# A two-layer diffusion block on one core: scan operands transposed ahead, the two scan directions in step, a last projection with fewer columns, and routing by halves

## The chip, the core and the metric

The kernel runs on one core of a Trainium2 chip. The metric is the device time of one execution in microseconds (us). The core has a matrix engine (TensorE, PE in the profile, with PEld for its weight loads), VectorE (DVE), ScalarE (ACT), GpSimd (POOL), and SyncE (SP), which only issues DMAs here. Each engine runs its own instructions strictly in the order in which they are written and waits on semaphores for the others.

## What is computed

Two layers (`l` = 0, 1) over 256 context tokens and 1024 latent tokens of width 1024, all in float32. Each layer projects the normalised tokens with `w_in`, runs four mixers side by side (a short convolution, an attention, a two-way RWKV scan and a two-way retention), projects back with `w_out`, and then sends each token set through 16 experts, each of which picks its own tokens. After the last layer only the latent tokens are returned, so there `need_ctx` is false: of the context, only what the mixers carry over to the latent tokens matters. The parts that the change touches, cut from the reference:

```python
def step(s, inp):                         # the scan, per token, in both directions
    w_t, a_t, k_t, v_t, kk_t = inp[:5]
    s = (s * w_t - einsum('bhvk,bhk->bhv', s, kk_t) * (kk_t * a_t) + v_t * k_t)
    y = einsum('bhvk,bhk->bhv', s, inp[5]) if emit else None

s_fw, yc_fw = wkv_scan(s0, *dc[0], vc, kkc, rc, False, need_ctx)   # context first
_, yx_fw = wkv_scan(s_fw, *dx[0], vx, kkx, rx, False, True)        # then the latent tokens

aff = softmax(hs @ w_router + b_router)   # routing
gate, idx = lax.top_k(aff.T, cap)         # cap = 128 of 1024 latent, 32 of 256 context
```

## The kernel before

Tokens lie in 10 tiles of 128 (`NT`): tiles 0 and 1 are context (`NCT` = 2), 2 to 9 latent. A stage is one block; all engines meet at its end. A layer is: norm, `stage_project`, attention, retention, and twice (for `p` = 0, 1, two heads each) `stage_rwkv_prep`, `stage_rwkv_scan`, `stage_rwkv_out`; then `stage_out`, `stage_topk`, `stage_moe`.

**Projection.** A job is one output tile, eight matmuls deep. Of groups "conv" and "rwkv" the weights are stationary and the tokens stream past in three spans (256, 512, 512 columns). Of group "tok" the tokens are stationary and 272 or 512 weight columns stream past, a job for each of the 10 token tiles. ACT evacuates even jobs, DVE odd ones. DVE also mixes each rwkv tile with its neighbours in time (`mix`, L553 to L562): `mix(i)` is written after the last job that DVE evacuates of tile `i + 1`, and `mix(7)` ends the stage. Both layers do the same jobs.

**Preparation of the scan.** Its tail is a loop of 15 rounds over both directions: a matmul against a constant (`spread`, L1343) copies 16x16 block rows across partitions, and DVE multiplies and subtracts (L1427, L1432) to invert these blocks. DVE waits for the matmuls, PE only for its ring of banks.

**Scan.** For each of 10 tiles and each direction `d` there are two kinds of work. The *inversion* of a tile needs no state: `products` (PE), `masked` (DVE, writes `UM`), the masks `NL` (POOL), `transposes` (PE, L1546: four operands by token, 16 small matmuls against the identity), `by_token` (ACT, copies them to `TM`), then twice `level_x` (PE), `x_out` (ACT), `level_t` (PE and DVE), and at last `w1_w2` (PE) and `w_out` (ACT, L1702 and L1704). The *carry* of the tile before takes the state through two halves of 64 tokens: `carry_u` and `carry_s`, each PE then DVE. `products` of the next tile waits for `w_out`, since they share banks. The order is written by hand: a tile takes 7 slots, and direction 1 runs 3 slots behind direction 0.

```python
SLOTS, LAG = 7, (0, 3)
def slots():
    for q in range(SLOTS * (NT + 1) + LAG[1]):
        yield [(d, *divmod(q - LAG[d], SLOTS)) for d in DD if 0 <= q - LAG[d] < SLOTS * (NT + 1)]
```

`level_x` waits for three signals: the mask of POOL, the block inverse in `TS`, and `tme`, the copy of ACT (`by_token`).

**Routing.** `g.aff` holds the affinities as 16 experts by 1280 tokens. `stage_topk` takes the 128 largest of 1024 in 16 rounds on DVE, each of which finds the 8 largest, finds their places and strikes them out. In layer 0 it then takes 32 of the 256 context tokens in 4 rounds. PE turns indices and values, and DVE copies them to `g.tok` and `g.gate`. In the same stage SP issues the loads of the first 8 expert weight parts (2 MB each).

## Time and profile before

| | us |
|---|---|
| median of three runs | 4874.7 (4870.68 to 4875.51) |
| the profiled execution | 4870.7 |
| its span, first to last instruction | 4868.8 |
| projection of layer 1 (PE, first to last matmul) | 2641.5 to 3099.3 |
| the four scans | 118.9, 118.9, 119.2, 120.5 |
| DVE in the rounds of routing, layer 0 / layer 1 | 1612.7 to 1681.0 / 4086.8 to 4148.8 |

A float32 matmul runs as two records in the trace, so 8 matmuls are "x16"; a transpose of 128x128 runs as one. A duration of a record ("mean ns of one") holds its latency as well; what PE spends on one in a row of many is their busy time by their count, or the distance of two starts. Rows of a timeline are start, duration, engine, line and tiles, and in brackets how long the engine had been idle and whose result ended that.

### The profile page before, as it was taken

To read this page: it belongs to the slowest core of one execution; us is meant where nothing else is said; L and a number is where in the kernel's file an instruction comes from. 1 tells how busy PE (TensorE), PEld (TensorE's weight loads), DVE (VectorE), ACT (ScalarE), POOL (GpSimd) and SP (SyncE) were. 2 spreads that over 40 slices of the span, in tenths; PEclk is the share of its full clock that TensorE was granted. 3 is DMA by queue.
4 is the path that set the end of the run, shared out by engine and by line. 5 is a ranking of instruction groups with operands and counts; after the bars stand their busy time and mean duration, and the time that the engine had idled before them with its cause. 6 is when DMAs were issued, how large, how long until landed. Compare 5 with 4: busy or idle time off the path is not lost. (4 is left out here: it accounts for less than half of the span.)

```text
span 4868.8 us, 64424 instructions
## 1 busy us (share of the span) xinstructions
PE 4017.1 (83%) x27764; PEld 2253.6 (46%) x27764; DVE 1579.1 (32%) x3277; ACT 793.1 (16%) x1792; POOL 450.7 (9%) x662
## 2 busy tenths in 40 slices
PE   6999688457779399999996999677466885899999
PEld 3645245445644144444443655344454742344444
DVE  2101454765633600000002101454666536100000
ACT  2000243133211000000002010243133210000000
POOL 0000100021200000001000000100021200000000
PEclk8999889688889599999997999789678987899999
DMA  4110400100045466677753110000100034688884
GB/s 151 62 72 11 138 34 10 50 20 16 3 176 222 171 229 229 243 264 259 262 186 84 59 71 16 26 3 22 45 12 16 3 126 181 240 312 309 311 327 161
DMA packets 196074, 624.94 MB, mean 128 GB/s; under 512 B 34473, under 2 KB 47017, under 8 KB 189137
## 3 DMA queue, kind: packets, MB, share of 16 engines
q1 hardware_dynamic: 173200, 548.13, 30.1%
q0 software_dynamic: 22592, 72.69, 4.9%
q8 instruction: 221, 3.62, 0.3%
q14 instruction: 61, 0.49, 0.0%
HBM read 566.90 MB, written 53.89 MB: 128 GB/s over the span
## 5 line engine op out<-in xcount | busy, mean ns | idle before, releaser
L484 PE MATMUL ps<-hT,p_w 128*128 128x512 f32 (+1 forms) x1344 | 486.2, 525 | 19.2 <-DMA p_w<-in_w_in_dram 19.2
L2177 PE MATMUL ps<-moe_w,e_xT 128*128 128x512 f32 x1024 | 451.2, 599 | 0.8 <-ACT e_xT L2239 0.8
L2214 PE MATMUL ps<-moe_w,e_hT 128*128 128x512 f32 x1024 | 445.9, 593 | 6.1 <-ACT e_hT L2258 6.1
L2184 PE MATMUL ps<-moe_w,e_xT 128*128 128x512 f32 x1024 | 444.7, 592 | 0.0
L487 PE MATMUL ps<-p_w,hT 128*128 128x272 f32 (+1 forms) x1280 | 422.3, 492 | 0.0
L484 PEld LDWEIGHTS ps<-hT,p_w 128*128 128x128 f32 x1344 | 258.1, 192 | 246.0 <-issue 213.3
L487 PEld LDWEIGHTS ps<-p_w,hT 128*128 128x128 f32 x1280 | 243.2, 190 | 178.9 <-issue 154.0
L2280 DVE TENSOR_TENSOR e_hid<-e_hid,ps 128x512 f32<-128x512 f32 x64 | 44.0, 688 | 838.6 <-PE ps L2184 838.6
L2177 PEld LDWEIGHTS ps<-moe_w,e_xT 128*128 128x128 f32 x1024 | 195.0, 192 | 247.2 <-issue 245.9
L2184 PEld LDWEIGHTS ps<-moe_w,e_xT 128*128 128x128 f32 x1024 | 194.6, 190 | 244.9 <-issue 244.9
L2214 PEld LDWEIGHTS ps<-moe_w,e_hT 128*128 128x128 f32 x1024 | 192.0, 190 | 239.0 <-issue 239.0
L1881 PE MATMUL ps<-o_w,yT 128*128 128x512 f32 x576 | 261.2, 608 | 29.6 <-DMA o_w<-in_w_out_dram 24.5
L860 PE MATMUL ps<-mla_KT,mla_QT 96*128 96x512 f32 (+1 forms) x400 | 181.8, 540 | 6.6 <-ACT a_pr L984 4.6
L1881 PEld LDWEIGHTS ps<-o_w,yT 128*128 128x128 f32 x576 | 109.3, 194 | 166.2 <-issue 133.1
L2290 DVE SCALAR_TENSOR_TENSOR e_ye<-ps,all_gate,e_rows 128x1024 f32<-128x1024 f32 x32 | 41.1, 1283 | 427.2 <-PE ps L2214 427.2
L2251 ACT ACTIVATE e_hid<-ps 128x512 f32<-128x512 f32 x64 | 34.7, 594 | 716.4 <-PE ps L2177 716.4
L570 DVE COPY p_zo<-ps 128x272 f32<-128x272 f32 (+1 forms) x40 | 22.7, 566 | 366.7 <-PE ps L487 366.7
L872 PEld LDWEIGHTS ps<-all_tabs,a_pr 128*128 128x128 f32 x656 | 74.4, 142 | 127.6 <-issue 86.6
L872 PE MATMUL ps<-all_tabs,a_pr 128*128 128x128 f32 x656 | 111.4, 283 | 19.3 <-ACT a_pt L929 13.8
L950 DVE TENSOR_REDUCE a_mx<-ps 128x1 f32<-128x1280 f32 (+1 forms) x72 | 98.5, 1368 | 54.4 <-PE ps L860 54.4
L2193 PE MATMUL ps<-moe_w,e_xTc 128*32 128x512 f32 x1024 | 113.2, 594 | 0.0
L2049 PE MATMUL ps<-all_tabs,k_idf 16*128 16x16 f32 (+1 forms) x3 | 0.8, 257 | 132.2 <-DVE k_idf L2034 132.2
(328 smaller groups left out, 5555.1 us busy)
## 6 DMA issues: line engine op xcount, KB each, us to landing
moe_w<-in_w_gate_dram SPq DMA_DIRECT2D x64, 2048.0 KB, 13.3
moe_w<-in_w_up_dram SPq DMA_DIRECT2D x64, 2048.0 KB, 11.0
moe_w<-in_w_down_dram SPq DMA_DIRECT2D x64, 2048.0 KB, 16.9
o_mod_w<-in_w_ada_dram SPq DMA_DIRECT2D x24, 1024.0 KB, 11.1
p_w<-in_w_in_dram SPq DMA_DIRECT2D x10, 2048.0 KB, 8.0
m_mod_w<-in_w_ada_dram SPq DMA_DIRECT2D x16, 1024.0 KB, 6.6
z_rows<-p_zo POOLq DMA_DIRECT2D x40, 256.0 KB, 2.3
r_z<-z_rows SPq DMA_DIRECT2D x20, 512.0 KB, 3.3
```

Source lines behind the costliest of these rows:

```text
L484: ins = nc.tensor.matmul(ps[:, j % NB, 0:tw], w[:, n % RW, k, m * P:(m + 1) * P], hT[:, k, t0:t0 + tw], start=(k == 0), stop=(k == KT - 1))
L487: ins = nc.tensor.matmul(ps[:, j % NB, 0:wd], hT[:, k, m * P:(m + 1) * P], w[:, n % RW, k, 0:wd], start=(k == 0), stop=(k == KT - 1))
L860: ins = nc.tensor.matmul(ps[:, SB[u % 2] + i, 0:w], QT[0:QK, h, t * P:(t + 1) * P], KTr[0:QK, h, n:n + w], start=True, stop=True)
L872: ins = nc.tensor.transpose(ps[:, TB, k * P:(k + 1) * P], pr[:, u % NP, (k0 + k) * P:(k0 + k + 1) * P], g.ident)
L950: link(nc.vector.reduce_max(mx[:, s % 2, 0:1], src, AX_X))
L1881: ins = nc.tensor.matmul(ps[:, 2 * (n % 2) + half, :], yT[:, k, t * P:(t + 1) * P], w[:, k, half * 512:(half + 1) * 512], start=(k == 0), ...
L2177: ins = nc.tensor.matmul(ps[:, c, :], xT[:, 4 * half + k], wp[:, k, c * 512:(c + 1) * 512], start=(half == 0 and k == 0), stop=(half == 1 ...
L2184: ins = nc.tensor.matmul(ps[:, 2 + c, :], xT[:, 4 * half + k], wp[:, k, c * 512:(c + 1) * 512], start=(half == 0 and k == 0), stop=(half = ...
L2193: ins = nc.tensor.matmul(ps[32 * q:32 * q + 32, 4, :], xTc[:, 4 * half + k], (wg, wu)[q // 2][:, k, (q % 2) * 512:(q % 2 + 1) * 512], star ...
L2214: ins = nc.tensor.matmul(ps[:, 6 + c, :], hT2[:, 4 * half + k], wp[:, k, c * 512:(c + 1) * 512], start=(half == 0 and k == 0), stop=(half ...
L2280: nc.vector.tensor_tensor(hid[:, h], hid[:, h], ps[:, 2 + c], ALU.mult).then_inc(*hd.up())
L2290: nc.vector.scalar_tensor_tensor(ye[:, e % 2], bank(ps, 6, D), g.gate[:, 0, e:e + 1], rows[:], ALU.mult, ALU.mult).then_inc(*yd.up())
```

## The change

Three parts, which touch no common stage.

**Projection of the last layer.** With `need_ctx` false, context tokens are left out where nothing reads them. The first span (256 columns) falls away for all 6 conv tiles and for rwkv tiles 0, 1 and 7. In the "tok" groups the two context tiles lose group 2 whole, keep 160 of 272 columns in group 3, and 256 of 512 in groups 4 and 5. POOL writes zeros into the context part of the conv tiles. `mix` takes the last job of its tile, wherever that is.

**Scan.** The four operands by token (three for direction 1; it shares the fourth) are made by 70 full transposes of 128x128 in the tail of the preparation, between the spread matmuls, into `BYTOK`, which lies where buffers of the preparation are free by then; ACT copies them out, 20 copies. In the scan `transposes` and `by_token` are gone, and both directions go through the same six slots together. `decayed` and `y_out` are written apart from the carries.

**Routing.** The affinities lie in rows of 512: the two halves of the latent tokens on partitions 0 to 15 and 32 to 47, the context on 64 to 79. The 16 rounds run on all of these rows at once; the 4 context rounds are gone. Then PE turns values and indices, the second half's list is reversed by a matmul against `flip`, and DVE merges the two lists with a maximum and a choice by comparison.

```diff
+    ctx_cols = {2: None, 3: (112, 272), 4: (256, 512), 5: (0, 256)}
+    ctx_tiles = range(2, 7)
...
-            jobs += [(n, m, s) for m in range(w // P) for s in range(3)]
+            jobs += [(n, m, s) for m in range(w // P) for s in range(3) if s or need_ctx or (kind == "rwkv" and o + m in ctx_tiles)]
...
-                    last = rw0 + 3 * i + 2
+                    last = max(j for j in range(rw0, len(jobs)) if tile_of(j) == i)
...
+            def by_token(u):
+                d, t = units[u]
+                if u >= 4:
+                    pe.wait_ge(*tok_out.at(u - 3))
+                for a, src in enumerate(sources(d)):
+                    ins = nc.tensor.transpose(ps[:, TBANKS[u % 4], a * P:(a + 1) * P], src[:, t * P:(t + 1) * P], g.ident)
+                ins.then_inc(*turned.up())
...
+                for u in range(len(units) * n // (DB - 1), len(units) * (n + 1) // (DB - 1)):
+                    by_token(u)
...
+            act.wait_ge(*ksd.at(1))
+            for u, (d, t) in enumerate(units):
+                act.wait_ge(*turned.at(u + 1))
+                w = len(sources(d)) * P
+                nc.scalar.copy(BT[d][:, t].rearrange("p a n -> p (a n)"), ps[:, TBANKS[u % 4], 0:w]).then_inc(*tok_out.up())
...
-                for now in slots():
...
+                for s in range(NT + 1):
+                    inv, car = s < NT, s > 0
+                    for d in DD:
+                        if car:
+                            w1_w2(d, s - 1)
+                    for d in DD:
+                        if inv:
+                            products(d, s)
+                        if car:
+                            carry_u(d, s - 1, 0)
+                    for d in DD:
+                        if inv:
+                            m_v(d, s)
+                        if car:
+                            carry_s(d, s - 1, 0)
+                        if inv:
+                            level_x(d, s, 0)
+                    for d in DD:
+                        if inv:
+                            level_t(d, s, 0)
+                        if car:
+                            carry_u(d, s - 1, 1)
+                    if inv:
+                        level_x(0, s, 1)
+                    if car:
+                        carry_s(0, s - 1, 1)
+                    if inv:
+                        level_x(1, s, 1)
+                        level_t(0, s, 1)
+                    if car:
+                        carry_s(1, s - 1, 1)
+                    if inv:
+                        level_t(1, s, 1)
...
+                for r in range(CAPX // 8):
+                    v8 = val[:, 8 * r:8 * r + 8]
+                    link(nc.vector.max(v8, a))
+                    link(nc.vector.max_index(idx[:, 8 * r:8 * r + 8], v8, a))
+                    link(nc.vector.match_replace(a, v8, a, -1.0))
...
+                nc.vector.tensor_tensor(g.gate[:, 0], tt[:, 0, A], ps[:, 1, 0:NE], ALU.max)
+                link(nc.vector.tensor_tensor(sel[:], tt[:, 0, A], ps[:, 1, 0:NE], ALU.is_ge))
+                link(nc.vector.tensor_tensor(dif[:], tt[:, 1, A], ps[:, 1, NE:2 * NE], ALU.subtract))
+                link(nc.vector.tensor_tensor(dif[:], dif[:], sel[:], ALU.mult))
+                link(nc.vector.tensor_tensor(dif[:], dif[:], ps[:, 1, NE:2 * NE], ALU.add))
+                nc.vector.tensor_copy(g.tok[:, 0], dif[:])
```

PE in the middle of a scan, before: `w1_w2` and the levels of one direction among the carries and transposes of the other (L1546 the transposes, L1556 `level_x`, L1574 `level_t`, L1537 `products`, L1524 and L1527 `carry_s`, L1509 and L1513 `carry_u`).

```order
L1537 MATMUL ps<-rw_KR,rw_BK 64x128 x8
L1556 MATMUL ps<-s_TS,s_NL 64x64 x4
L1524 MATMUL ps<-s_UM,s_TM 64x64 x2
L1527 MATMUL ps<-s_TM 64x64 x2
L1524 MATMUL ps<-s_UM,s_U 64x64 x2
L1527 MATMUL ps<-s_U,s_TM 64x64 x2
L1546 MATMUL ps<-all_tabs,rw_KR 64x64 x4
L1546 MATMUL ps<-all_tabs,rw_BK 64x64 x8
L1546 MATMUL ps<-all_tabs,M 64x64 x4
L1574 MATMUL ps<-s_TS,s_X 64x64 x4
```

The same engine and place after the change (L1571 `products`, L1543 and L1547 `carry_u`, L1588 `m_v`, L1558 and L1561 `carry_s`, L1580 `level_x`; `rp_wide` holds the operands by token).

```order
L1571 MATMUL ps<-rw_KR,rw_BK 64x128 x8
L1543 MATMUL ps<-s_S,s_W 64x64 x2
L1547 MATMUL ps<-rw_KR,s_S 64x64 x2
L1588 MATMUL ps<-rp_wide,s_UM 64x64 x4
L1558 MATMUL ps<-s_UM,rp_wide 64x64 x2
L1561 MATMUL ps<-rp_wide 64x64 x2
L1558 MATMUL ps<-s_UM,s_U 64x64 x2
L1561 MATMUL ps<-s_U,rp_wide 64x64 x2
L1580 MATMUL ps<-s_TS,s_NL 64x64 x4
L1588 MATMUL ps<-rp_wide,s_UM 64x64 x4
```

The transposes are gone, and the second direction's `m_v` now stands right behind the first direction's `level_x`.

PE in the tail of the preparation, before: the spread matmuls stand in a row.

```order
L1331 MATMUL ps<-rw_KR,rw_BK 32x32 x160
L1343 MATMUL ps<-rp_GX,rp_SG 128x300 x2
L1343 MATMUL ps<-rp_GX,rp_SG 128x280 x2
L1343 MATMUL ps<-rp_GX,rp_SG 128x260 x2
L1343 MATMUL ps<-rp_GX,rp_SG 128x240 x2
```

The same place after the change (L1374 the spread matmuls, L1341 the transposes).

```order
L1374 MATMUL ps<-ro_GX,ro_SG 128x300 x2
L1341 MATMUL ps<-all_tabs,rw_KR 128x128
L1341 MATMUL ps<-all_tabs,rw_BK 128x128 x2
L1341 MATMUL ps<-all_tabs,M 128x128
L1374 MATMUL ps<-ro_GX,ro_SG 128x280 x2
L1341 MATMUL ps<-all_tabs,rw_KR 128x128
L1341 MATMUL ps<-all_tabs,rw_BK 128x128 x2
L1374 MATMUL ps<-ro_GX,ro_SG 128x260 x2
```

Between two pairs of spread matmuls there are now three to seven transposes.

## Rows read from the trace of the kernel before

**Rows 1.** Groups by line and shape, 2580 to 3120 us; count, busy us, mean ns
```profile
L484 PE MATMUL ps<-hT,p_w 128*128 128x512 f32 x448 | 194.5, 592 | 0.0
L487 PE MATMUL ps<-p_w,hT 128*128 128x512 f32 x320 | 137.7, 592 | 0.0
L487 PE MATMUL ps<-p_w,hT 128*128 128x272 f32 x320 | 73.7, 392 | 0.0
L484 PE MATMUL ps<-hT,p_w 128*128 128x256 f32 x224 | 52.8, 390 | 9.6 <-DMA p_w<-in_w_in_dram 9.6
```
**Rows 2.** Timelines of PE and of DVE at the end of layer 1's projection
```profile
2961.68 137.66 PE L484 MATMUL ps<-hT,p_w 128*128 128x256 f32 x384
...
3107.24 1.28 DVE L561 SCALAR_TENSOR_TENSOR M<-p_z,p_omu,p_tmp 128x1024 f32<-128x1024 f32 x1
```
**Rows 3.** Stretches of a scan: length, busy us by engine, clock share (1.00 is 2.4 GHz)
```profile
1080.00:1156.00 76.00, 64.68 (x2201) 59.63 (x2199) 44.60 (x154) 27.98 (x96) 20.58 (x56) 1.00 0.02 4
1049.00:1052.00 3.00, 1.92 (x47) 1.76 (x48) 0.45 (x2) 0.65 (x2) 1.42 (x4) 0.50 0.00 0
```
**Rows 4.** Timeline of DVE: the same instruction of one direction, one tile apart
```profile
1098.38 0.69 DVE L1647 TENSOR_TENSOR s_UM<-ps,rw_masks 128x512 f32<-128x512 f32 x1
...
1109.36 0.69 DVE L1647 TENSOR_TENSOR s_UM<-ps,rw_masks 128x512 f32<-128x512 f32 x1
```
**Rows 5.** Timeline of the engines from that mask to the first level
```profile
1099.15 0.87 POOL L1695 TENSOR_TENSOR s_NL<-s_UM,rw_nlev 128x128 f32<-128x128 f32 x2 [2.35 <-DVE s_UM L1647]
...
1099.89 0.59 ACT L1709 COPY s_TM<-ps 128x512 f32<-128x512 f32 x1 [0.54 <-PE ps L1546]
...
1100.62 0.45 PE L1556 MATMUL ps<-s_TS,s_NL 64*64 64x64 f32 x8 [0.35 <-ACT s_TM L1709]
```
**Rows 6.** Timeline of PE in a scan: starts of bursts that follow one another
```profile
1101.64 0.44 PE L1586 MATMUL ps<-s_MV,s_TS 64*64 64x64 f32 x8
1101.87 0.44 PE L1574 MATMUL ps<-s_X,s_TS 64*64 64x64 f32 x8
...
1103.07 0.33 PE L1537 MATMUL ps<-rw_KR,rw_BK 64*64 64x128 f32 x3
...
1103.57 0.44 PE L1556 MATMUL ps<-s_TS,s_NL 64*64 64x64 f32 x8
1103.84 0.33 PE L1524 MATMUL ps<-s_UM,s_TM 64*64 64x64 f32 x4
...
1104.24 0.28 PE L1527 MATMUL ps<-s_U,s_TM 64*64 64x64 f32 x4
```
**Rows 7.** Timeline of ACT: the last copies of w_out
```profile
1102.30 0.53 ACT L1704 COPY s_W<-ps 64x128 f32<-64x128 f32 x2
```
**Rows 8.** Timeline of DVE: the last update of the state in the first scan
```profile
1166.24 0.28 DVE L1633 SCALAR_TENSOR_TENSOR s_S<-ps,rw_ET,s_Se 128x64 f32<-128x64 f32 x1 [1.22 <-PE ps L1527]
```
**Rows 9.** Timelines of PE and DVE: start and end of the preparation's loop
```profile
1029.55 1.37 PE L1343 MATMUL ps<-rp_GX,rp_SG 128*128 128x300 f32 x2
...
1047.08 0.32 DVE L1432 TENSOR_TENSOR rw_TD<-rw_TD,rp_GX 128x20 f32<-128x20 f32 x2
```
**Rows 10.** Timeline of PE: eight transposes at the full clock, in the experts
```profile
4189.27 1.04 PE L2158 MATMUL ps<-all_tabs,e_xe 128*128 128x128 f32 x8
```
**Rows 11.** A stretch of layer 1's norm, where PE only transposes
```profile
2620.00:2630.00 10.00, 6.86 (x30) 5.26 (x28) 7.34 (x22) 9.13 (x22) 2.20 (x4) 0.50 0.29 101
```
**Rows 12.** Instructions on the affinities: duration ns min/median/max
```profile
L2030 DVE MAX8 k_val<-all_aff x36: 407/1216/1217, 1612.7 to 4144.9; 16x8 f32<-16x1024 f32 x32, 16x8 f32<-16x256 f32 x4
```
**Rows 13.** Timeline of DVE in layer 1's routing: one round, and the end
```profile
4086.75 1.22 DVE L2030 MAX8 k_val<-all_aff 16x8 f32<-16x1024 f32 x1 [0.32 <-PEq L1831]
...
4090.62 1.22 DVE L2030 MAX8 k_val<-all_aff 16x8 f32<-16x1024 f32 x1
...
4149.84 0.17 DVE L2038 COPY all_gate<-ps 128x16 f32<-128x16 f32 x1
```
**Rows 14.** A stretch of layer 1's routing; last two numbers: DMA share, GB/s
```profile
4125.00:4130.00 5.00, 0.00 (x0) 0.00 (x0) 4.86 (x7) 0.00 (x0) 0.00 (x0) 0.50 0.92 365
```

264 lines of the change are left out of this document (140 added, 124 removed).

## The prediction

> **What bounds the kernel now.** I read the busy shares in 40 slices first: PE is nearly full in both projections and both expert stages and lower between them, and the three parts of the change lie in stages that share nothing. So each of the three parts is costed in its own stage. Next come the groups by shape in the projection: PE streams without a gap, 434 ns for a record of 512 columns, 230 ns for one of 272 [rows 1]. Whatever columns go, their time goes. Then the stretches inside a scan: in 76 us PE is busy for 64.7, DVE for 44.6, at the full clock of 2.4 GHz [rows 3]. Neither is full; the same mask instruction of one direction comes back after 10.98 us, so a tile of both directions takes that long [rows 4]. Last the routing: DVE works alone there, and PE waits.
>
> **Projection of layer 1.** Removed are 9 jobs of 256 columns, 16 records each: 144 records. The group of 256 gives 52.8 / 224 = 236 ns, but it holds the cold start; from the 384 records of the rwkv groups, 137.66 us [rows 2], take 256 of 512 columns at 434 ns, and 128 are left with 26.6 us, 207 ns each. I take 215: 31.0 us. Two jobs of 272 columns: 32 x 0.230 = 7.4. Four jobs halved from 512: 64 x (0.430 - 0.215) = 13.8. Two jobs from 272 to 160: by columns a record would take 135 ns, and not less than the 110 of a full transpose below; I take 160, so 32 x 0.07 = 2.2. Sum 54.4 (50 to 58). The end shortens too. Before, DVE's last job was the last of all, and behind it stood both `mix(6)` and `mix(7)`: PE ends at 3099.3 and DVE at 3108.5 [rows 2], 9.2 us. Now the count of jobs is odd, DVE's last job lies one job (6.9 us) earlier, `mix(6)` (4.1 us) runs beneath PE's last job, and only `mix(7)` and a copy stay: about 4.9 us, 4.3 less. The zeros that POOL writes lie at the stage's start, before anything asks for them. **Projection: -58.7 us.** Its cover is nothing; PE is the bound.
>
> **The scan's step.** What goes is the transposes with their copy. The first level could start once POOL's first mask is there, half of 0.87 us after 1099.15, at 1099.6; it starts at 1100.62, having waited for ACT's copy, 0.59 us, which waited for the transposes [rows 5]. So each inversion loses 1 us of chain. What is late next is PE itself. The bursts' prices by the distance of starts [rows 6]: eight records of a level or of `m_v` 0.23 to 0.27, `products` 0.50, `carry_s` 0.52 (12 records in 0.40, and 4 more), `carry_u` 0.25, `w1_w2` 0.41 (half of it on four quarters of the array, half as a level). One direction of one tile now holds `w1_w2` 0.41, `products` 0.50, two `carry_u` 0.50, `m_v` 0.24, two `carry_s` 1.04, two `level_x` 0.54, `level_t` 0.47 and 0.24: 3.94 us. Both: 7.9 us, and a step can't be shorter. To that come the waits in PE's new order. The largest is at `products`: `w1_w2` of direction 0 must end (0.2 us behind its last start), ACT copies `w_out` in about 0.73 (0.53 of it the two last copies [rows 7]), and beneath it lies only `w1_w2` of direction 1: PE stands 0.4 to 0.6 us. I went through a step with these prices, 0.2 us from a burst's last start to its end and 0.05 us for each handover: elsewhere the other direction's burst covers each wait (for `masked` 0.69, for U, for X 0.27), with 0.1 left over here and there, and DVE, with 3.6 us for each direction, is just in time for `w1_w2` of direction 1. That gives 8.5; I take 8.6. From 10.97 to 8.6 are 2.37 us, for 9 full steps of 4 scans: 85.3 us.
>
> **The scan's ends.** The first scan runs from 1047.4 to 1166.5, 119.1 us [rows 8, 9]; less 9 steps of 10.97 its two ends take 20.4. The lag of 3 slots, 4.7 us, is part of it. New: a first step of inversions alone, at the half clock (0.50 in its second to fourth us [rows 3]), some 9.5 us, and a last one of carries alone, some 7: 16.5. Four times 3.9 is 15. **Scans: -100 us** (bounds: step 8.0 gives -122, step 9.4 gives -71).
>
> **The preparation's tail.** Added are 70 transposes of 128x128 per scan. Eight take 1.04 us with their latency [rows 10], so 0.11 each: 7.7 us of PE. The spread matmuls stream 4 records x 20 x (1 + ... + 15) = 9600 columns; at 0.434 / 512 = 0.85 ns that is 8.1 us, and 9.2 if the short ones cost no less than a transpose. Together 17 us at the full clock. The loop took 17.9 us with DVE as its bound, 1029.5 to 1047.4, and started at the half clock: its first two records, 300 columns each, take 1.37 us [rows 9]. With some 4 us of such a start PE needs about 20.5 us and becomes the bound. Behind it stands one copy of ACT (0.59 as in [rows 5]); the 20 copies, some 11 us, lie beside PE, and ACT is idle there. I take +4 per scan (0 to +14). **Preparation: +16 us.** The copies wait for POOL's sum of keys too, which is over ten us earlier.
>
> **Routing.** One round takes 4090.62 - 4086.75 = 3.87 us [rows 13]. The search takes 0.407 us on 256 columns and 1.216 on 1024 [rows 12], so by a straight line 0.68 on 512; the other two are alike. A round of 512 then takes 3.87 - 3 x 0.54 = 2.26, provided that 80 partitions cost as much as 16: the row says only that the time follows the columns. 16 rounds: -25.8 us in each layer. Layer 0 also loses its 4 context rounds, 5.9 us. Sixteen rounds end at 4148.7 and the copies at 4150.0 [rows 13], 1.3 us; now PE turns, DVE copies, PE reverses, and six small steps follow, about 3.5 in all; +2.2 in each layer, less 0.6 of separate context copies in layer 0, and three memsets ahead, +0.3. Layer 0: -29.5; layer 1: -23.3. SP's loads of weights start with the stage as before, behind one more small DMA, and still run until 4130 in layer 1 [rows 14]; the first gather would now start at 4126 and share the last 4 us with them, +1. **Routing: -51.8 us.**
>
> **The sum.** 4870.7 (the profiled execution, 4.0 below the median of the three) - 58.7 - 100 + 16 - 51.8 = 4676.2. I predict 4676.
>
> **Rivals.** (a) *PE alone sets the step.* The wait for `w_out` is filled by running ahead; step 7.9, 36 x 0.7 = 25 less: 4651. For it: PE can have its next burst ready. Against: `products` really needs the banks that `w_out` reads. (b) *A slot keeps its length.* 10.97 / 7 = 1.57 us; six are 9.4: +29, 4705. For it: in step both directions ask DVE for the same thing at once, and DVE would be at 7.2 of 9.4 us. Against: the slots before held the transposes, which were their longest wait. (c) *The tail of the preparation runs at 1.2 GHz.* In a stretch of layer 1's norm where PE only transposes, it is busy for 6.86 of 10 us and the granted clock stays at 0.50 [rows 11], where as busy a scan has 1.00 [rows 3]. If the transposes between them thin out the spread matmuls so far that the clock stays down, PE needs 2 x 17 us from its start at 1029.5, to 1063: +16 instead of +4; with part of the loop at the full clock I price it at +10 over the forecast in each, +40: 4716. For it: that row. Against: the spread matmuls alone have raised the clock so far, with gaps between them. The Trainium skill says in "TensorE: Matmul & The Clock Gate", Part 4, that a transpose in transpose mode doesn't count as PE being busy; by that rule, the norm's row agrees, and rival (c) would be what happens. (d) *The scan stays at 1.2 GHz.* Its first steps do, with both directions at work (0.50 [rows 3]). Were it to last, PE's 7.9 us would be 15.8 and a step 16.4: 36 x 7.8 = 281 more, 4957, slower than before. It decides from a step of 14.0 us on, where 36 x 5.4 eats the whole gain. Against: PE issues for nine tenths of a step, more than before. That the change doesn't do what it says could hold for the narrow jobs only (a record of 160 or 256 columns as dear as one of 272): +3.
>
> **How the numbers follow.** The forecast 0.58; (a) 0.10; (b) 0.15; (c) 0.10; (d) 0.02; something between or a mishap of a few us elsewhere 0.05. The range has (a) and the step of 8.0 near its lower end and (b) and most of (c) near its upper: 4645 to 4718. All but (d) lie far below 4870, so faster has 0.97, slower 0.02, and within 0.2% (about what a measurement of this kernel can tell from no change) 0.01.
>
> **What would show it.** In the trace after: the mask of one direction comes back after 8.6 us (7.9, 9.4 or over 14 for the rivals); the wait of `level_x` for ACT is gone, and the largest waits of PE in a scan stand at `products` for `w_out`; the loop of the preparation ends 4 us later, with the granted clock at 1.00 in its middle (0.50 by (c)); DVE's MAX8 takes 0.68 us; PE's stretch in layer 1's projection is 54 us shorter. Wrong would be made most easily the step, since 36 of them stand in the sum: each 0.1 us is 3.6.

## The result and the profile after

The changed kernel takes 4644.9 us (median of 4 runs, 4635.1 to 4646.2), beside 4875.1 for the kernel before in the same series: a ratio of 0.9523, 95% interval 0.9507 to 0.9540. The prediction was 4676 with a range of 4645 to 4718, so the time lies 31 us below the forecast and 0.1 us below the range's lower end. A second series gave 4632.8 (5 runs, 4629.3 to 4640.4) beside 4872.5, 0.9512 (0.9499 to 0.9525). So the direction and three of the four terms held, and the fourth, the scans, gave 37 us more than priced.

The profiled execution is the run of 4645.8 us, 224.9 less than that of before. By stage (us, from DVE's and PE's timelines of both traces):

| part | predicted | measured | from |
|---|---|---|---|
| projection of layer 1 | -58.7 | -59.7 | PE's stretch 457.9 to 402.4, its end 9.2 to 5.0 |
| the steps of the scans | -85.3 | -107 | step 10.97 to a mean of 7.99, 36 of them |
| the ends of the scans | -15 | -30 | 20.5 to 13.1, four of them |
| the preparation's tail, with the gap to the scan | +16 | +15.1 | +3.6, +3.3, +5.6, +2.7, from the end of DVE's last product of the preparation to the scan's first instruction |
| routing | -51.8 | -49.6 | layer 0 -27.9, layer 1 -21.8 |
| everything else | 0 | +6.3 | the largest are the output stage of layer 0 (+4.1) and the attention of layer 1 (+3) |

**The projection.** Timelines of PE and of DVE at its end, after; they answer to [rows 2].

```profile
2835.01 127.30 PE L494 MATMUL ps<-hT,p_w 128*128 128x512 f32 x336
```
```profile
2955.53 0.69 DVE L582 COPY p_z<-ps 128x512 f32<-128x512 f32 x1 [8.88 <-PE ps L494]
...
2963.02 1.50 DVE L570 TENSOR_TENSOR p_tmp<-p_z 128x1282 f32<-128x1282 f32 x1 [2.63 <-ACT p_z L514]
...
2965.99 1.28 DVE L573 SCALAR_TENSOR_TENSOR M<-p_z,p_omu,p_tmp 128x1024 f32<-128x1024 f32 x1
```

PE ends at 2962.3 and DVE at 2967.3. DVE waits 2.63 us for ACT before the last `mix`: `mix(6)` lies beneath PE's last job and only `mix(7)` is left, 5.0 us where 9.2 stood.

**The scan's step.** Timeline of DVE, after, the mask of direction 0 one tile apart, as in [rows 4].

```profile
1101.44 0.68 DVE L1688 TENSOR_TENSOR s_UM<-ps,rw_masks 128x512 f32<-128x512 f32 x1
...
1109.38 0.65 DVE L1688 TENSOR_TENSOR s_UM<-ps,rw_masks 128x512 f32<-128x512 f32 x1
```

7.94 us, where 10.98 stood. In the four scans half of the steps with y take 7.91 to 7.96, the others 7.97 to 8.55; the four steps of layer 1's scans whose tiles have no y take 7.62. The mean of all, without each scan's first, is 7.99. How full the engines are in it (length, busy us of PE, PEld, DVE, ACT, POOL, granted clock, DMA):

```profile
1085.00:1125.00 40.00, 38.60 (x1276) 36.68 (x1274) 33.29 (x110) 14.28 (x60) 14.37 (x40) 1.00 0.02 5
```

PE is busy for 97% of it where [rows 3] had 85%, DVE for 83% (6.7 us of a step) where it had 59%. The handover that the prediction priced highest, `products` waiting for `w_out`, in the timelines of ACT and PE:

```profile
1099.94 0.27 ACT L1758 COPY s_W<-ps 128x128 f32<-128x128 f32 x1 [0.93 <-PE ps L1611]
1100.11 0.53 ACT L1760 COPY s_W<-ps 64x128 f32<-64x128 f32 x2
1100.66 0.27 ACT L1758 COPY s_W<-ps 128x128 f32<-128x128 f32 x1
```
```profile
1099.49 0.41 PE L1611 MATMUL ps<-s_MV,s_TS 64*64 64x64 f32 x8
1099.92 0.34 PE L1607 MATMUL ps<-s_TS,rp_wide 64*64 64x64 f32 x8
1100.08 0.41 PE L1611 MATMUL ps<-s_MV,s_TS 64*64 64x64 f32 x8
1100.69 0.67 PE L1571 MATMUL ps<-rw_KR,rw_BK 64*64 64x128 f32 x16 [0.20 <-ACT s_W L1760]
```

The last line's bracket is the wait: 0.20 us, and 0.17 to 0.20 in each step (1.7 us over nine of them). It counts from the modelled end of the last record. By the distance of starts, in which the prediction's prices stand, `products` begins 0.77 us behind the first record of `w1_w2(1)`, where 0.48 pass if nothing is waited for (rows of e14 below): PE stands 0.29 us. ACT starts 0.04 us behind the end of `w1_w2(0)`, 0.26 behind its last start, and frees the banks after 0.70.

**The scan's ends.** The first step runs from 1052.7 to 1060.5, 7.8 us, where 9.5 was priced for it at the half clock. The rows show why (stretches, after; columns as above):

```profile
1052.70:1055.70 3.00, 1.89 (x50) 1.52 (x52) 2.22 (x6) 0.27 (x1) 1.86 (x6) 1.00 0.00 0
1055.70:1060.50 4.80, 4.31 (x118) 3.59 (x114) 1.90 (x7) 2.02 (x9) 1.74 (x6) 1.00 0.02 3
```

In [rows 3] the clock stood at 0.50 there. Now PE comes from a loop that it fills (4.73 of the last 5 us) at 2.4 GHz and keeps it. In the third scan it falls for a while (0.61 from 3462 to 3465), and there the first step is 1 us longer than in the other three. The last step, carries alone, takes some 5.3 us where 7 was priced.

**The preparation.** Stretches of the loop's start in the first scan's preparation, before and after:

```profile
1032.00:1034.00 2.00, 2.00 (x6) 1.45 (x5) 1.31 (x4) 0.00 (x0) 0.00 (x0) 0.50 0.00 0
1034.00:1036.00 2.00, 2.00 (x10) 1.60 (x8) 1.72 (x6) 0.00 (x0) 0.00 (x0) 0.87 0.00 0
```
```profile
1034.00:1036.00 2.00, 2.00 (x8) 1.70 (x7) 1.23 (x3) 0.59 (x1) 0.00 (x0) 0.50 0.00 0
1036.00:1038.00 2.00, 2.00 (x9) 1.56 (x8) 1.45 (x4) 0.37 (x1) 0.00 (x0) 0.64 0.00 0
1038.00:1040.00 2.00, 2.00 (x15) 1.79 (x14) 1.92 (x6) 1.08 (x3) 0.00 (x0) 1.00 0.01 4
```

The loop starts at 1029.6 and at 1031.1. The clock reaches 2.4 GHz 5.0 us into it before and 6.3 us after; in its middle it is 1.00, as the forecast wanted. In the other three preparations it rises 5.4, 5.1 and 4.0 us into the loop before and 4.7, 6.6 and 4.4 after.

Ahead of the loop, inside the small matmuls of the second diagonal block, PE stands for up to 2.1 us without a releaser. The row before:

```profile
1029.25 0.37 PE L1331 MATMUL ps<-rw_KR,rw_BK 64*32 64x32 f32 x17 [1.89 <-issue]
```

In the four preparations this idle time is 1.89, 0, 0 and 0.14 us before and 2.07, 0.50, 2.15 and 0 after. What it is stayed open; with it the loops start 2.6 us later in sum behind DVE's last product, and that is in the +15.1.

**Routing.** Groups by shape in layer 0, after, which answer to [rows 12]:

```profile
L2097 DVE MAX8 k_val<-all_aff 80x8 f32<-80x512 f32 x16 | 11.1, 691 | 0.5
L2098 DVE FIND_INDEX8 k_idx<-k_val,all_aff 80x8 uint32<-80x512 f32 x16 | 10.9, 680 | 0.0
L2099 DVE MATCH_REPLACE8 all_aff<-k_val,all_aff 80x512 f32<-80x512 f32 x16 | 10.7, 671 | 0.0
```

0.69 us by the trace against 0.68 by the straight line; layer 1, with 48 partitions, has 0.685. A round takes 2.30.

### The profile page after: what moved, and what is told of

It reads as the page before. It is cut to its first block and busy times, and to the rows that moved or that the text cites. A ratio compares the mean times of both kernels' runs of the same rounds, so it can differ in the third digit from the quotient of the medians.

```text
span 4644.0 us, 59628 instructions
## 1 busy us (share of the span) xinstructions
PE 3916.4 (84%) x25314; PEld 2193.2 (47%) x25314; DVE 1537.9 (33%) x3265; ACT 785.5 (17%) x1787; POOL 450.5 (10%) x661
## 5 line engine op out<-in xcount | busy, mean ns | idle before, releaser
L494 PE MATMUL ps<-hT,p_w 128*128 128x512 f32 (+1 forms) x1200 | 454.4, 541 | 19.9 <-DMA p_w<-in_w_in_dram 19.9
L497 PE MATMUL ps<-p_w,hT 128*128 128x272 f32 (+3 forms) x1248 | 398.3, 481 | 0.0
L494 PEld LDWEIGHTS ps<-hT,p_w 128*128 128x128 f32 x1200 | 229.7, 192 | 243.4 <-issue 214.3
L582 DVE COPY p_zo<-ps 128x272 f32<-128x272 f32 (+3 forms) x39 | 21.6, 553 | 343.8 <-PE ps L497 343.8
L1362 PE MATMUL ps<-rw_KR,rw_BK 64*32 64x32 f32 x1280 | 15.8, 245 | 110.2 <-DVE rw_BK L1445 103.4
## 6 DMA issues: line engine op xcount, KB each, us to landing
o_mod_w<-in_w_ada_dram SPq DMA_DIRECT2D x24, 1024.0 KB, 10.6
```

The source lines that it names most:

```text
L494: ins = nc.tensor.matmul(ps[:, j % NB, 0:tw], w[:, n % RW, k, m * P:(m + 1) * P], hT[:, k, t0:t0 + tw], start=(k == 0), stop=(k == KT - 1))
L497: ins = nc.tensor.matmul(ps[:, j % NB, 0:hi - lo], hT[:, k, m * P:(m + 1) * P], w[:, n % RW, k, lo:hi], start=(k == 0), stop=(k == KT - 1))
```

## The experiments

Each time is a median of 4 or 5 runs (10 for one), each ratio is to the kernel before in the same series, with its 95% interval. The series differ by some 12 us for the same kernel (see the result), so that small differences are read from the traces: the four scans' lengths, their steps (from mask to mask of one direction) and the preparation's tails (from the end of DVE's last product of the preparation to the scan's first instruction).

### One part alone: e1, e2

Only the narrower projection, on the kernel before (from the diff, what `stage_project` takes):

```diff
-                        stage_project(nc, g, I, l, M)
+                        stage_project(nc, g, I, l, M, need_ctx)
```

> The kernel before with the narrower projection of layer 1 alone. By the traces of before and after the stage itself gives 59.7 us (55.4 of PE's stretch, 4.2 of its end). If the stages are independent, the time is 4875 - 59.7 = 4815. The kernel after is some 6 us slower elsewhere than the parts explain, 3 of them in the attention of layer 1, behind this stage: if the narrower projection causes that, the time is 4818 and the attention of layer 1 is 3 us longer in this trace.

Measured 4810.5 us, 0.9877 (0.9859 to 0.9896), 61 us less than before. The stage takes 406.2 us in its trace from the first matmul to the last `mix`, 465.7 before: 59.5 less. The attention (first score matmul to the first of the retention) takes 206.3 us, 203.3 before.

Only routing in halves (`stage_topk`, the layout of the affinities, the reversing matrix):

```diff
-        g.aff = fixed("aff", [NE, T])
+        g.aff = fixed("aff", [64 + NE, SEQ // 2])
```

> The kernel before with routing in halves alone. By the traces the two routing stages give 27.9 and 21.8 us: 4875 - 49.7 = 4825. Between the end of the second scan and the first MAX8 the kernel after takes 2.8 us longer; if that belongs to this part, 4828. The searches should show 0.68 us on 80 partitions in layer 0 and on 48 in layer 1. If the time of a search depended on the partitions too, the two layers would differ.

Measured 4825.8, 0.9900 (0.9882 to 0.9918), 48 us less. The attention takes 206.5 us here too, in a kernel without the narrower projection, so these 3 us come from neither part. Over all runs of this study that stretch varies from 201.3 to 208.3, the output stage of layer 0 from 185.2 to 191.8, and the stretch from layer 1's retention to its first preparation's tail from 160.5 to 167.2, in kernels that don't differ there. The kernel after itself had 167.2 in its first profile and 160.5 in its second. So the +6.3 us "elsewhere" lie within such variation, and a cost of the change there can't be told from it.

### The two halves of the scan's change: e3, e4

The old order (seven slots, direction 1 three behind), with the operands turned ahead:

```diff
-                for s in range(NT + 1):
-                    inv, car = s < NT, s > 0
+                for now in slots():
+                    for d, s, i in now:
...
-                        if i == 2 and s < NT:
-                            transposes(d, s)
```

> The kernel after, with the scan in its old order (seven staggered slots, direction 1 three slots behind), the operands turned in the preparation as in after. It tells what removing the transposes gives by itself. Theory 1 (PE's issue sets the step, and any order that keeps PE fed reaches it): the step is 8.0 to 8.4, the ends are as long as before (20 instead of 13), so 4645 + 4 x 7 + 36 x 0.2 = 4680. Theory 2 (working in step is what fills PE's waits; staggered, a slot keeps its 1.57 us less the transposes' half microsecond in one slot of each direction): the step is 9.5 to 10, 4645 + 28 + 36 x 1.8 = 4738.

In step, with the operands turned inside each step:

```diff
+                    for d in DD:
+                        if inv:
+                            transposes(d, s)
```

> The kernel after, in step in six slots, but with the operands turned inside each step as in the kernel before (16 small matmuls for each direction behind the products, and ACT's copy of 0.59 us), nothing turned in the preparation. Theory 1 (PE's issue sets the step): 8.0 + 2 x 0.5 = 9.0, and the copies are covered by the other direction; the preparation's tail is 15 us shorter in all: 4645 - 15 + 36 x 1.0 + 4 x 1.5 = 4672. Theory 2 (the copy stands in the chain of each direction, and in step both directions wait for it at once): the step is 10 or more, 4645 - 15 + 72 + 8 = 4710 or more.

| | scans, sum | step | tails, sum | time |
|---|---|---|---|---|
| before | 476.8 | 10.97 | 82.6 | 4875.1 |
| turned ahead only (e3) | 403.8 | 9.28 | 98.8 | 4705.7, 0.9659 (0.9634 to 0.9685) |
| in step only (e4) | 412.4 | 8.9 to 11.0, mean 9.8 | 87.5 | 4694.2, 0.9635 (0.9617 to 0.9652) |
| both (after) | 339.8 | 7.99 | 97.7 | 4644.9, 0.9523 (0.9507 to 0.9540) |

In e3 most steps agree to 0.1 us, 0.2 us under theory 2's, and the time lies between the theories' 4680 and 4738. In e4 they swing, which stayed unexplained; the mean and the time lie between the theories' too. In the scans turning alone gives 73.0 us, working in step alone 64.4, and both together 137.0: they add up to within 0.5 us. Neither the transposes nor the order was the one price of the old step, and neither needs the other for its gain.

### What sets 8.0 us: e5, e6, e7, e13, e14, e15

Less on PE: the y part of `carry_s` is left out.

```diff
-                        if has_y(d, s):
+                        if False:
                             for h in range(2):
                                 nc.tensor.matmul(ps[HALF[h], CA[d] + c, Yc], right[HALF[c], HALF[h]],
```

> The kernel after without the part of the output y that carry_s adds (the four matmuls of 64x64 into the y columns in each burst with y; the state is computed as before, y is not). It takes 4 x 8 = 32 records, some 0.9 to 1.0 us by the distance of starts, off PE in a step, and nothing off the chain from state to state but a quarter microsecond in each of two bursts. Theory 1 (PE's issue sets the step of 8.0): the step falls to 7.0 to 7.2, 4645 - 33 x 0.9 = 4615 (steps with y only). Theory 2 (the chain of the inversion, products to w_out, sets it and PE has just kept pace): the step stays within 0.2 of 8.0, 4640 or more.

Measured 4620.8, 0.9493 (0.9473 to 0.9514); the step is 7.62, hardly ever another, in all four scans. 32 records are gone and 0.3 to 0.4 us, a third of their price: neither theory.

More on ACT, in `w_out`:

```diff
+                    for c in range(2):
+                        nc.scalar.copy(W3[d][HALF[c]], ps[HALF[c], LV[d] + c, CH:3 * CH])
```

> The kernel after with two more copies of ACT in w_out (the two of 64x128, 0.26 us each, once more into tiles that nobody reads, ahead of the real ones): w_out is 0.53 us longer for each direction. ACT is busy for 3 of 8 us, so only the wait of products for w_out can show it. Theory 1 (that wait is real, 0.17 us now, and nothing else lies beneath the copies than w1_w2 of direction 1): it grows by 0.53 for direction 0, and products of direction 1 has its own after that, since ACT serves the directions in turn: step 8.0 + 0.5 to 1.06, 4645 + 18 to 38. Theory 2 (PE's step has room elsewhere that takes the delay up, as a wait that ends earlier later on): within 5 us of 4645.

Measured 4685.4, 0.9616 (0.9600 to 0.9632); step 8.92, 1.0 more. PE's timeline shows where:

```profile
1107.19 0.67 PE L1572 MATMUL ps<-rw_KR,rw_BK 64*64 64x128 f32 x16 [0.72 <-ACT s_W L1763]
1108.45 0.67 PE L1572 MATMUL ps<-rw_KR,rw_BK 64*64 64x128 f32 x16 [0.38 <-ACT s_W L1763]
```

The first `products` waits 0.72 where it waited 0.20, the second 0.38 where it didn't wait. Theory 1 at its upper end.

More on DVE: `masked` twice.

```diff
+                    link(nc.vector.tensor_tensor(UM[d][:, s % 2].rearrange("p h a n -> p h (a n)"), ps[:, LV[d]:LV[d] + 2, 0:4 * CH],
+                                                 R["masks"][:, d].rearrange("p a n -> p (a n)").unsqueeze(1).broadcast_to([P, 2, 4 * CH]),
+                                                 ALU.mult))
```

> The kernel after with DVE's masked (0.66 us, of 128x512) done twice for each direction and step: 1.33 us more of DVE, which is busy for 6.7 of 8.0 us now, and 0.66 more in the chain of each direction. Theory 1 (PE's issue alone sets the step): DVE at 8.0 of 8.0 would only just keep up, step 8.1 to 8.3, 4645 + 4 to 11. Theory 2 (DVE and the chain of the inversion are level with PE, which the step of 7.62 without the y part of carry_s points to): 8.0 + 0.7 to 1.3, 4645 + 25 to 47.

Measured 4698.3, 0.9646 (0.9630 to 0.9662); step 9.36: 1.45 more for 1.33 us of instructions: theory 2, and more than it had.

So additions on ACT and DVE, two of PE's suppliers, cost their full length. The other way round, less on DVE (half of the mask), less on ACT (one copy of `w_out`), and less on DVE and PE at once:

```diff
+                    na = 4 if s < 2 else 2
-                    nc.vector.tensor_tensor(UM[d][:, s % 2].rearrange("p h a n -> p h (a n)"), ps[:, LV[d]:LV[d] + 2, 0:4 * CH],
+                    nc.vector.tensor_tensor(UM[d][:, s % 2, :, 0:na].rearrange("p h a n -> p h (a n)"), ps[:, LV[d]:LV[d] + 2, 0:na * CH],
```

> The kernel after with DVE's masked done on the first half of its columns only, from the third step of each scan on (the masks of the other two products are left out, the old values stand there). It takes about 0.27 us off DVE for each direction and step, and as much off the chain from products to the next burst. Adding 0.66 to the same place cost 1.32 us a step. Theory 1 (PE's issue is the floor of the step; DVE and ACT have just kept pace): the step loses at most the 0.1 to 0.2 us that PE stands in it, 4645 - 4 = 4641. Theory 2 (the step is a chain through DVE's mask): the step falls by 0.4 to 0.54 us, 28 steps, 4645 - 11 to 15 = 4632.

```diff
-                    for c in range(2):
+                    for c in range(2 if s < 1 else 1):
                         ins = nc.scalar.copy(W2[d][HALF[c]], ps[HALF[c], LV[d] + c, CH:3 * CH])
```

> The kernel after with the second copy of W2 left out of ACT's w_out from the second step on (the old values stand there): 0.25 us less for each direction in front of products. Adding 0.53 to the same place cost 0.9 us a step. Theory 1 (PE's issue is the floor, and PE stands 0.17 us a step for w_out of direction 0): the step loses 0.15 to 0.2 us, 4645 - 6 = 4639. Theory 2 (products of both directions wait for ACT in turn, so that the copies stand in the step in full): it loses 0.4 us or more, 4645 - 14 = 4631.

> The kernel after without the y part of carry_s on PE (as in the kernel that had the step of 7.62) and with the half mask on DVE from the third step on. Theory 1 (without those 32 records PE is no longer the bound, and a chain through DVE's mask sets 7.62): the step falls to 7.1 to 7.2. Theory 2 (7.62 is PE's issue still, the records left out having cost half of what the distance of starts says): the step stays above 7.5.

| | time | ratio | most frequent step |
|---|---|---|---|
| after | 4644.9 / 4632.8 | 0.9523 / 0.9512 | 7.91 |
| half the mask (e13) | 4633.4 | 0.9505 (0.9489 to 0.9521) | 7.69 |
| one copy less (e14) | 4635.3 | 0.9511 (0.9493 to 0.9529) | 7.91 |
| no y part (e5) | 4620.8 | 0.9493 (0.9473 to 0.9514) | 7.62 |
| no y part, half the mask (e15) | 4615.5 | 0.9463 (0.9446 to 0.9479) | 7.29 |

Taking 0.25 us from ACT gives nothing at all, adding 0.53 costs 1.0: the copies were just covered. Taking 0.27 from each mask gives 0.22 with the y part and 0.33 without it; taking 32 records from PE gives 0.3, and 0.4 when the mask is halved too. In e13, e14 and e15 each result lies between or beside the two theories, so no theory of one bound holds. PE's own issue is at most 7.7 us (it gets a step done in that), not 7.9; waits for the masks that are shorter than a record's latency of 0.22 us stand in no row.

Why the shorter `w_out` gave nothing stands in e14's trace. Timelines of POOL, PE and DVE in it:

```profile
1089.79 1.20 POOL L1744 TENSOR_TENSOR s_TS<-rw_TD,rw_dmask 128x64 f32<-128x64 f32 x4 [3.64 <-PE ps L1611]
```
```profile
1089.74 0.34 PE L1607 MATMUL ps<-s_TS,rp_wide 64*64 64x64 f32 x8
1090.22 0.67 PE L1571 MATMUL ps<-rw_KR,rw_BK 64*64 64x128 f32 x16
...
1091.97 0.39 PE L1588 MATMUL ps<-rp_wide,s_UM 64*64 64x64 f32 x6 [0.24 <-DVE s_UM L1688]
```
```profile
1091.03 0.31 DVE L1694 STREAM_TRANSPOSE s_TS<-s_TS 128x128 f32<-128x128 f32 x1 [0.22 <-POOL s_TS L1744]
1091.26 0.65 DVE L1688 TENSOR_TENSOR s_UM<-ps,rw_masks 128x512 f32<-128x512 f32 x1
```

And in after:

```profile
1099.99 1.18 POOL L1744 TENSOR_TENSOR s_TS<-rw_TD,rw_dmask 128x64 f32<-128x64 f32 x4 [3.99 <-PE ps L1611]
```
```profile
1101.21 0.31 DVE L1694 STREAM_TRANSPOSE s_TS<-s_TS 128x128 f32<-128x128 f32 x1 [0.21 <-POOL s_TS L1744]
```

There is a third supplier. Behind `w1_w2(0)` POOL writes the block inverses of both directions into `TS`, 1.20 us; DVE transposes them, waits for POOL before the second, and only then masks. In e14 `products` waits for nothing and ends 0.38 us ahead of the mask, where after has 0.11, but the mask still starts 1.47 us behind POOL's first instruction, as in after, and now `m_v` waits 0.25 us for it (medians of 32 steps). So the wait of `products` for `w_out`, the largest in PE's rows, isn't in the step: what the mask waits for is POOL. In after the mask and PE's own order are level to some 0.05 us at `m_v(0)`; in e13 the mask ends early enough and PE is the later. No run shortens POOL's four instructions, so what they are worth stayed untested. The step is a balance in which PE, the chain through POOL and DVE, and ACT's copies are late at once.

### Why PE needs less than the bursts' sum

Part of this stands in the starts of PE's records. Timeline of PE, after, around `m_v(0)` (L1588) and the first `carry_s(0)` (L1558), which stands behind it in the program:

```profile
1093.90 0.53 PE L1588 MATMUL ps<-rp_wide,s_UM 64*64 64x64 f32 x5
1094.18 0.27 PE L1558 MATMUL ps<-s_UM,rp_wide 64*64 64x64 f32 x1
1094.27 0.22 PE L1588 MATMUL ps<-rp_wide,s_UM 64*64 64x64 f32 x2
1094.29 0.22 PE L1558 MATMUL ps<-s_UM,rp_wide 64*64 64x64 f32 x1
1094.32 0.22 PE L1588 MATMUL ps<-rp_wide,s_UM 64*64 64x64 f32 x1
```

A record of the later burst starts at 1094.18, three records of the earlier one at 1094.27 and after. `m_v` alternates between the two row halves of the array and `carry_s` uses one of them; the later burst begins in its half while the other is still being served. The Trainium skill says in "TensorE: Matmul & The Clock Gate", Part 3, that matmuls keep the program's order in start and end; by these starts they don't, across row halves, and the measurement decides. The prices by the distance of starts [rows 6] may thus hold a burst's neighbours in them. Their sum, 7.9, was at least 0.2 too high by e13's steps of 7.69, although `w1_w2`, priced at 0.41, takes 0.48 by e14's rows; how much of this the overlap makes wasn't measured.

### All four quarters at once: e9

```diff
+                    if car:
+                        pair(s_parts, smm, s - 1, 0)
...
+                    for i in range(max(size)):
+                        for d in DD:
+                            if i < size[d]:
+                                ins = lists[d][i]()
```

> The kernel after with the carries of the two directions issued in pairs, matmul by matmul: at each moment direction 0 uses one half of the array's rows and direction 1 the other (their chunks run in opposite order), so all four quarters work. By the distance of starts a record costs 30 ns over two quarters and 17 over four, so 96 records a step cost some 1.2 us less. Theory 1 (PE's issue sets the step): 8.0 - 1.2 = 6.8, 4645 - 43 = 4602. Theory 2 (without PE's load the chain sets 7.6, as without the y part): 4645 - 14 = 4631. Theory 3 (each pair has to wait for the later direction, and that takes more than the quarters give): a step over 8.0, 4650 or more.

Measured 4680.5, 0.9606 (0.9590 to 0.9622): slower than after by 36 us, and by 40 if the ratios are compared; theory 3. Timeline of PE:

```profile
1101.52 0.34 PE L1637 MATMUL ps<-s_UM,rp_wide 64*64 64x64 f32 x8 [0.16 <-DVE s_U L1704]
1101.65 0.33 PE L1640 MATMUL ps<-rp_wide 64*64 64x64 f32 x8
1101.77 0.33 PE L1637 MATMUL ps<-s_UM,s_U 64*64 64x64 f32 x8
1101.88 0.33 PE L1640 MATMUL ps<-s_U,rp_wide 64*64 64x64 f32 x8
```

The quarters do what was hoped: 32 records in 0.48 us, 15 ns each, where each direction alone took about 0.5. But the pair can't start before the later direction's U, the mask of direction 1 comes 1.4 us behind the other instead of 0.8, and the steps with y take 8.6 to 9.7. PE is busy for 35.2 of 40 us instead of 38.3. The fullest engine gets through the same work sooner, and the kernel is slower: what it had was cover.

### The preparation and the clock: e8, e10, e11, e12

Six of the twenty turnings ahead of the loop, where PE waits for DVE:

```diff
+    EARLY = (4, 2)
...
+                for u in range(sum(EARLY[:d]), sum(EARLY[:d + 1])):
+                    by_token(u)
```

> The kernel after with six of the twenty turnings of the preparation (24 of 70 transposes, direction 0's first six tiles) ahead of the loop: four between the diagonal blocks of the two directions, where PE stands 3.8 us for DVE, and two behind the second, where it stands 2.1. The loop then holds 46 transposes. Theory 1 (PE bounds the preparation's tail): the loop loses 24 x 0.11 to 0.21 us, the tail is 2.5 to 3.5 us shorter in each scan: 4645 - 12 = 4633. Theory 2 (the loop is as long by its slow start at 1.2 GHz and DVE's chain, 18 to 19 us; or the early transposes push the diagonal blocks of direction 1 back): 0 to -3 us, 4642 or more.

Measured 4619.0, 0.9484 (0.9467 to 0.9501). Tails 19.7, 22.1, 19.9, 19.6: 81.4 in all where after has 97.7, 16.3 us less. The 24 records at 0.11 us make 10.6 in the four loops, so the same number was issued at the same places for nobody, with the 70 left in the loop:

```diff
+                for u in range(4 if d == 0 else 2):
+                    for a, src in enumerate(sources(0)):
+                        nc.tensor.transpose(ps[:, (0, 1, 2, 5)[u], a * P:(a + 1) * P], src[:, (u + 4 * d) * P:(u + 4 * d + 1) * P], g.ident)
```

> The kernel after with 24 transposes more in each preparation, at the places where the kernel with early turnings has its 24 (16 between the two diagonal blocks, 8 behind the second), into banks that the loop overwrites; nobody reads them, and the loop keeps its 70. That kernel took 5.2, 0.5, 5.2 and 2.1 us off the four tails and saw the granted clock at 1.00 from 1028.7 on, where after has it from about 1037. Theory 1 (half of that gain is the clock, which rises earlier because PE is busy before the loop): the tails are 2 to 3 us shorter than in after in scans 1 and 3, 4645 - 7 = 4638, with the clock at 1.00 when the loop starts. Theory 2 (all of it is the work taken out of the loop): tails as in after or up to 1.7 us longer, 4645 to 4652, and the clock rises as in after.

Measured 4625.4, 0.9488 (0.9470 to 0.9506), with more work than after. Tails 22.1, 21.1, 21.0, 22.7: 86.9, so 10.8 of e8's 16.3 us come without any work leaving the loop (7.7 of 13.2 against the second profile of after, whose tails make 94.6). Theory 1, and more than it had: 3.7 and 4.9 us in the first and third. Timeline of PE and stretches:

```profile
1024.62 0.63 PE L1369 MATMUL ps<-all_tabs,rw_BK 128*128 128x128 f32 x2
1025.04 0.34 PE L1369 MATMUL ps<-all_tabs,M 128*128 128x128 f32 x1
1025.22 0.27 PE L1369 MATMUL ps<-all_tabs,rw_KR 128*128 128x128 f32 x1
1025.33 0.38 PE L1369 MATMUL ps<-all_tabs,rw_BK 128*128 128x128 f32 x2
1025.55 0.27 PE L1369 MATMUL ps<-all_tabs,M 128*128 128x128 f32 x1
```
```profile
1024.00:1026.00 2.00, 1.82 (x11) 1.58 (x9) 1.97 (x2) 0.00 (x0) 0.00 (x0) 0.71 0.00 0
1026.00:1028.00 2.00, 1.27 (x127) 1.18 (x128) 1.93 (x6) 0.00 (x0) 0.00 (x0) 1.00 0.04 8
```

The starts go from 0.21 us apart to 0.11 at 1025.1: the clock rises from 1.2 to 2.4 GHz in the midst of a row of transposes, with only the small matmuls of the diagonal blocks ahead of them. It is at 1.00 when the loop starts and stays there. The same in the kernel before:

> The kernel before with the same 24 transposes in each preparation, read by nobody. There the loop has no transposes, DVE bounds it from its middle on, and the clock rises 5 us into it. Theory 1 (the early transposes raise the clock before the loop starts): the loop's first records run at full clock, the tails are 1.5 to 2.5 us shorter, 4875 - 7 = 4868. Theory 2 (transposes leave the clock alone): unchanged or up to 1 us longer each, 4875 to 4879.

Measured 4872.7 (10 runs), 0.9996 (0.9987 to 1.0006). Stretch of its trace:

```profile
1024.00:1026.00 2.00, 1.53 (x89) 1.29 (x90) 1.96 (x4) 0.00 (x0) 0.00 (x0) 0.91 0.03 8
```

The clock rises there as well, 10 us earlier than in the kernel before, and the time doesn't change: the tails make 80.9 (before 82.6). That is not because the clock did nothing. Divided at the loop's first record (us, sums of the four preparations; the loop up to the scan's first instruction of any engine, 0.1 us ahead of DVE's):

| | from DVE's last product to the loop | the loops | clock at 1.00, from the loop's start |
|---|---|---|---|
| before | 10.2 | 72.0 | 4.0 to 5.4 behind |
| with 24 for nobody (e11) | 15.5 | 64.9 | 3.0 to 5.0 ahead; in the fourth it falls and comes back 1.8 behind |
| after | 12.8 | 84.5 | 4.4 to 6.6 behind |
| after again (e16) | 12.3 | 81.8 | 1.3 to 5.1 behind |
| with 24 for nobody (e10) | 12.9 | 73.6 | 1.6 to 4.8 ahead |
| six turned early (e8) | 16.9 | 64.0 | 1.9 to 4.4 ahead |
| ten turned early (e12) | 24.8 | 64.0 | 4.0 to 7.2 ahead |

In the kernel before the loops are 7.1 us shorter with the clock up, though DVE bounds them from their middle on; in after, which PE bounds, 10.9. But e11's loops start 5.3 us later: 8 of the transposes stand between the second diagonal block and the loop (0.93 us each time, 1.72 in the fourth at the half clock), and PE stands there for 0.22, 0.82, 0.98 and 2.08 us without a releaser. In e10 the same transposes stand there too, and the starts came out even because this idle time was shorter than in after (0.96 us in one preparation, against 4.7 in three): that part is luck. Ten turnings ahead of the loop:

```diff
-    EARLY = (4, 2)
+    EARLY = (4, 6)
```

> The kernel after with ten of the twenty turnings ahead of the loop (all of direction 0: four between the diagonal blocks, six behind the second), so 30 transposes stay in the loop. With six early ones the median was 4619. Theory 1 (PE still bounds the loop): 16 transposes less at 0.11, 1.5 us less in each scan, 4613. Theory 2 (DVE bounds the loop now, at 17.5 us): unchanged, 4617 to 4621. Theory 3 (the six behind the second diagonal block, with their four banks and ACT's copies of 0.5 us, hold up the loop's first record): 1 us more each, 4623.

Measured 4629.1, 0.9494 (0.9476 to 0.9513); tails 21.7, 24.1, 21.9, 21.6. Theory 3, and dearer than it had: 2 us each instead of 1. Theory 2 holds beside it: the loops take 64.0 us with 46 transposes and with 30, so PE no longer bounds them. In the first preparation DVE is ready for the loop at 1029.3, ACT's six early copies end at 1031.3, and the loop's first record starts at 1031.36.

### Beside each other: e16, e17, e18

> The kernel after once more, beside the next two on the same chip: 4640 to 4647.

Four instructions a step moved from DVE to ACT:

```diff
-                    link(nc.vector.tensor_scalar(Se[d][:], S[d][:, n % 3], scale_of(d, s, q), None, ALU.mult))
+                    nc.scalar.activation(Se[d][:], S[d][:, n % 3], ACT.Copy, scale=ET[d][:, 1, j:j + 1]).then_inc(*sd[d].up())
```

> The kernel after with the decayed state (Se, four instructions of 0.30 us in a step) computed by ACT instead of DVE: DVE busy for 5.5 of 8 us instead of 6.7, ACT 4.1 instead of 3.0. Nothing is left out. Theory 1 (DVE's queue makes up the part of the step that isn't PE's issue, as 0.27 us less for each mask gave 0.22 to 0.3): the step falls to 7.6 or 7.7, 36 x 0.25 = 9, 4636. Theory 2 (decayed runs in DVE's idle time, only the mask stands in the chain): the step stays at 7.9 and the time within 3 us. Theory 3 (ACT does them ahead of w_out and is late with it; 0.53 us more in that place cost 0.9): the step is over 8.0, 4655 or more.

> The same, with six turnings ahead of the preparation's loop (the version of 4619 us): 20 to 26 us under the run before it, by theory 1 some 4610, by theory 2 4617, by theory 3 over 4625.

| | time | ratio | most frequent step | tails |
|---|---|---|---|---|
| after again (e16) | 4632.8 | 0.9512 (0.9499 to 0.9525) | 7.91 | 94.6 |
| decayed on ACT (e17) | 4630.4 | 0.9506 (0.9493 to 0.9519) | 7.86 | 95.6 |
| and six turned early (e18) | 4618.8 | 0.9478 (0.9465 to 0.9491) | 7.86 | 81.7 |

A stretch of e17, to be read beside that of after:

```profile
1090.00:1130.00 40.00, 38.69 (x1298) 37.12 (x1293) 28.07 (x90) 20.18 (x84) 14.48 (x40) 1.00 0.02 5
```

DVE is busy for 28 of 40 us, 5 less, and the step falls by 0.05. Theory 2: what stands in the step is where DVE's mask lies, not how full DVE is; DVE waits 0.30 us for POOL instead of 0.23, and the mask starts 1.47 us behind POOL's first instruction as before. The kernel after came out 7 us under what was expected of it (4640 to 4647), and the early turnings are worth 11.6 us beside e17 on the same chip, not the 20 to 26 expected. So e8 and e18 beat both kernels, e18 by 14 us over after in the same series; by e10 about half of the loops' gain is the clock's (10.9 of 20.5 us).

Not tried: `w_out` in one copy, for which its two results would have to lie in one bank.

## Why the prediction was right or wrong

**The projection, right.** -59.7 against -58.7: 55.4 us of PE's stretch (54.4), 4.2 of the end (4.3). The part alone gave 61.

**Routing, right.** -49.6 against -51.8. The straight line through 256 and 1024 columns gave 0.68 and the trace has 0.69 for 80 and 0.685 for 48 partitions. The difference is in the round (2.30, not 2.26: 0.6 in each layer) and the rest behind the rounds; the terms given for layer 0 add up to -29.8, not -29.5. The gather behind layer 1's routing takes 9.35 us to the first copy, 8.18 before, and 8.7 to 9.4 in all traces with the new routing against 7.7 to 8.2 with the old: the +1 for its collision with the loads, which then fill the DMA engines (share 1.03 from 3925 to 3930). Layer 0's takes 0.9 longer as well, which had no term.

**The preparation, right in its sum, in part by luck.** +15.1 against +16. As reasoned, PE became the bound, and ACT's last copy stands in the gap (1.40 us, 0.40 before): the loops with the gap give +12.5 (+9.8 in the second profile). The other 2.6 lie ahead of the loop, where the forecast had nothing. Rival (c) was wrong about the clock: it rises 4.4 to 6.6 us into the loop, 4.0 to 5.4 before, and then stays. The rule that it named, of the Trainium skill in "TensorE: Matmul & The Clock Gate", Part 4, that transposes don't count as work there, doesn't hold for these: [rows 11] agreed with it at 0.50, e10 and e11 show the clock rising from transposes. Whether those run in the mode that the page speaks of, no row tells.

**The scan's step, wrong by 0.6 us: 22 of the 37.** The step that failed is the sum of the step: PE's bursts as a floor of 7.9 us, and on top of it "PE stands 0.4 to 0.6 us" at `products` with the small handovers. The wait is there, and is the largest of PE in a scan, but it is 0.29 us in the prediction's own units (0.20 in the rows; `w1_w2(1)` starts later than priced and covers more), and it adds nothing: in e14 it is gone and the step is 7.91 as before. The floor was too high: e13 does all of PE's work in 7.69. "Elsewhere the other direction's burst covers each wait" was wrong for the mask: it waits for POOL's 1.20 us behind `w1_w2(0)`, which the prediction had left out. In place of "7.9 plus the wait for `w_out`" the runs show PE and the chain through POOL and DVE level at 7.9, with ACT's copies just covered. Rival (a) named 7.9 and priced 4651; the step came out there, but not because PE alone sets it: e7 and e13 show DVE's mask in it with nearly its full length. Rival (b), that a slot keeps its length, fell: e3 keeps seven slots and they shrink from 1.57 to 1.33 when the transposes go. Rival (d) had no part in it.

**The scan's ends, wrong by 3.7 us each: 15 of the 37.** The term "a first step ... at the half clock, some 9.5 us" took the clock of [rows 3] over into a kernel in which PE comes from a full loop: it takes 7.8 at the full clock. The change to the preparation, costed as a loss by itself, paid for a part of this: two terms of the sum weren't independent. The last step was priced 1.7 too long.

**The range.** It ended at rival (a)'s price with the ends as forecast. The step and the ends both came out at their favourable bounds, and the range had joined them as if only one could. The 6.3 us elsewhere brought the first series back to its edge, which is luck; the second lies 12 us outside.
